# Sixteen units of one modulation matrix move from the first stage into a feed-forward

## The reference, cut to what matters

```python
def ada_params(cvec, w, b):                 # w_ada_2: 1024 x 9216, b_ada_2: 9216
    m = jax.nn.silu(cvec) @ w + b
    return m.reshape(cvec.shape[0], N_ADA, 1, D_MODEL)    # nine vectors of 1024

def half_ffn(h, shift, scale, gate, g_pre, g_post, w13, w2):
    u = modulate_2(rmsnorm_2(h, g_pre), shift, scale)
    return h + 0.5 * gate * rmsnorm_2(swiglu(u, w13, w2), g_post)
```

## Time and profile before

| | |
|---|---|
| median of the runs | 2324.3 us |
| the profiled execution's own time | 2324.03 us |
| its span | 2322.7 us |
| TensorE busy | 1988.2 us (86%) |
| VectorE busy | 1008.7 us (43%) |
| ScalarE busy | 735.0 us (32%) |
| GpSimd busy | 42.6 us (2%) |
| moved by DMA | 672.03 MB, mean 289 GB/s |
| mean granted TensorE clock | 0.93 |

### The profile page before, as it was taken

One profiled execution on the slowest core, in us unless ns is written; L12 is line 12 of the kernel. 1 busy time (PEld: TensorE's weight loads), 2 busy tenths in 40 slices (PEclk: granted clock), 3 DMA queues, 4 the chain that ended last, 5 costly groups with the idle time before them and its releaser, 6 DMA issues.

```text
span 2322.7 us, 28401 instructions
## 1 busy us (share of the span) xinstructions
PE 1988.2 (86%) x11830; PEld 1307.0 (56%) x11830; DVE 1008.7 (43%) x1713; ACT 735.0 (32%) x1196; POOL 42.6 (2%) x47
## 2 busy tenths in 40 slices
PE   6999877877877777877788789989999899999997
PEld 3646413433333333332444378868999788785786
DVE  3544222212222221222533277667664767653486
ACT  4323211101111111112210054454654554543365
POOL 0000000000000000000000000000000000000010
PEclk9999789899889998988889999999999999999999
DMA  9977999999999999999999965535345555350430
GB/s 390 414 306 266 408 377 413 414 413 414 413 414 416 415 413 415 414 411 409 414 403 410 410 207 181 186 102 169 113 141 177 164 178 186 98 199 19 145 119 19
DMA packets 210432, 672.03 MB, mean 289 GB/s; under 512 B 11504, under 2 KB 134512, under 8 KB 152192
## 3 DMA queue, kind: packets, MB, share of 16 engines
q1 hardware_dynamic: 210304, 670.21, 74.8%
HBM read 669.12 MB, written 1.05 MB: 289 GB/s over the span
## 4 chain that ended last, share of the span: by engine, by line
PE 50%; DMA 34%; DVE 11%; ACT 4%; issue 2%; SPq 0%; POOL 0%; DVEq 0%; ACTq 0%; POOLq 0%
DMA ring<-in_w 25%; PE pb L232 7%; PE pb L233 7%; PE pb L234 7%; PE pb L240 7%; DMA ring<-in_w_a 5%; PE pb L241 3%; PE pb L1852 3%; DVE WB L339 3%; DMA ring<-in_w_in 3%; PE pb L1877 2%; PE pb L782 2%; ACT WB L333 1%; DMA ring<-in_w_mod 1%; PE pb L1836 1%
## 5 line engine op out<-in xcount | busy, mean ns | idle before, releaser
L339 DVE TENSOR_TENSOR WB<-ring,WB 128x1024 fp32r<-128x1024 f32 (+3 forms) x370 | 426.1, 1193 | 463.9 <-ACT WB L333 463.6
L333 ACT ACTIVATE WB<-ring 128x1024 fp32r<-128x1024 f32 (+3 forms) x370 | 361.6, 1026 | 799.2 <-DMA ring<-in_w_a 466.0
L1852 PE MATMUL pb<-ring,big 128*32 128x512 f32 x2048 | 302.7, 684 | 139.9 <-DMA ring<-in_w 124.2
L232 PE MATMUL pb<-HHL,WB 128*128 128x256 f32 (+1 forms) x976 | 292.0, 299 | 11.7 <-DVE WB L339 4.3
L233 PE MATMUL pb<-HHL,WB 128*128 128x256 f32 (+1 forms) x976 | 283.0, 290 | 0.0
L234 PE MATMUL pb<-HHL,WB 128*128 128x256 f32 (+1 forms) x976 | 282.5, 289 | 0.0
L240 PE MATMUL pb<-HHL,WB 128*128 128x512 f32 x704 | 250.0, 400 | 1.9 <-DVE tmpT L649 1.5
L1852 PEld LDWEIGHTS pb<-ring,big 128*32 128x32 f32 x2048 | 47.3, 114 | 360.1 <-DMA ring<-in_w 268.3
L232 PEld LDWEIGHTS pb<-HHL,WB 128*128 128x128 f32 x976 | 194.0, 199 | 35.8 <-issue 21.3
L1877 PE MATMUL pb<-ring,big 128*32 128x512 f32 x1024 | 172.5, 673 | 48.4 <-DMA ring<-in_w 40.4
L241 PE MATMUL pb<-HHL,WB 128*128 128x256 f32 x704 | 197.3, 280 | 0.0
(11 more groups left out here) (467 smaller groups left out, 2265.0 us busy)
## 6 DMA issues: line engine op xcount, KB each, us to landing
ring<-in_w SPq DMA_DIRECT2D x384, 1024.0 KB, 16.4
ring<-in_w_a SPq DMA_DIRECT2D x66, 1024.0 KB, 13.2
ring<-in_w_in SPq DMA_DIRECT2D x38, 1024.0 KB, 10.2
ring<-in_w_ada SPq DMA_DIRECT2D x36, 1024.0 KB, 9.9
ring<-in_w_b SPq DMA_DIRECT2D x33, 1024.0 KB, 5.0
ring<-in_w_mod SPq DMA_DIRECT2D x24, 1024.0 KB, 12.0
ring<-in_w_out SPq DMA_DIRECT2D x8, 1024.0 KB, 6.3
ring<-in_b_w_in SPq DMA_DIRECT2D x8, 1024.0 KB, 6.4
```

Of the source, the lines that this page charges most:

```text
L232: pe.matmul(o, l[0], r[0], start=start, stop=False)
L333: act.activation(WB[:, c % 2, 0, x:y], flat[:, x:y], ACT.Copy).then_inc(*A(("high", c, z)))
L339: dve.tensor_tensor(WB[:, c % 2, 1, x:y], flat[:, x:y], WB[:, c % 2, 0, x:y].bitcast(F32), ALU.subtract).then_inc(*V(("low", c, z), *([("f ...
L1852: e = pe.matmul(PB[half][32 * j:32 * j + 32, :], xeT[:, kk, 32 * x:32 * x + 32], s[:, 512 * j:512 * j + 512], start=kk == 0, stop=kk == 7)
```

## The change

`w_ada_2`'s columns 0 to 5119 stay where they are: two vectors of 8 units and the 4 units of `TWO`, now columns 4096 to 5119. The other 4096 columns, 16 units of 128 rows, are loaded in `fa`, three behind every four chunks. ScalarE multiplies a unit in place by its rows' conditioning values (the first unit of each half straight into a total), GpSimd adds it to the total, and when all eight are in, TensorE sums the total over the partitions with a matrix of ones, ScalarE copies the bank, TensorE picks, and VectorE adds the bias and forms the scales. This is done twice, for two halves b of 2048 columns. A freed slot is now given back by GpSimd. In the attention's projection chunks the number of units behind a chunk is taken from `FILL`. The router's first bank changes from 6 to 3. The diff, cut to its core:

```diff
-    ADA = [("ada", nb) for nb in range(5)]
-    TWO = ("ada", 4)
+    ADA = [("ada", nb) for nb in range(3)]
+    TWO = ("ada", 2)
+    FILL = (1, 1, 1, 1, 2, 2, 1)
...
+    LATE_AT = {1 + 4 * k // 3: k for k in range(16)}
+
+    def sp_late(sp, t):
+        if t not in LATE_AT:
+            return
+        b, u = divmod(LATE_AT[t], 8)
...
+            load(sp, ("late", b, u), late_columns(b, u), 2048)
...
+    def late_total(b):
+        return ((big[:, 6656:8192], 0, 1536), (mraw[:, :], 1536, 2048)) if b else ((big[:, 3584:5632], 0, 2048),)
+
+    def act_late(act, t):
...
+        act.wait_ge(*landed(("late", b, u)))
+        if u:
+            act.activation(part, part, ACT.Copy, scale=cs[:, 1, u, 0:1]).then_inc(*A(("late", b, u)))
+            return
...
+    def pool_late(pool):
+        for b in range(2):
+            for u in range(1, 8):
+                pool.wait_ge(*at("late", b, u))
+                pool.wait_ge(*(at("late_total", b, u - 1) if u > 1 else at("late", b, 0)))
+                for total, x, y in late_total(b):
+                    pool.tensor_tensor(total, total, slot(("late", b, u))[:, x:y], ALU.add).then_inc(
+                        *G(*([("late_total", b, u), ("free", ("late", b, u))] if y == 2048 else [])))
+
+    def pe_late_sum(pe, b):
+        pe.wait_ge(*at("late_total", b, 7))
+        pe.wait_ge(*at("summed", "fa", 9 if b else 6, 0 if b else 1, 0 if b else 1))
+        for j in range(4):
...
+            e = pe.matmul(late_bank(b)[32 * j:32 * j + 32, :], ones[:, 0:32], total[:, 0:512] if b and j == 3 else total[:, 512 * j:512 * j + 512],
+                          start=True, stop=True)
+        e.then_inc(*P(("late_sum", b)))
+
+    def pe_late_pick(pe, b):
+        pe.wait_ge(*at("late_raw", b))
...
+    def act_late_raw(act, b):
+        act.wait_ge(*at("late_sum", b))
...
+        act.activation(fa.tmp[0], late_bank(b)[:, :], ACT.Copy).then_inc(*A(("late_raw", b)))
...
# attention, in all engines' programs
-                steps(g2, 3)
+                steps(g2, FILL[q - 1])
...
-            steps(g2, 3)
+            steps(g2, FILL[3 + q])
...
# sp_half
             load_chunk(sp, c)
+            if F is fa:
+                sp_late(sp, c - F.s0)
# pe_half
+                    if F is fa and (p, q, f) == (7, 1, 0):
+                        pe_late_sum(pe, 0)
+                    if F is fa and (q, f) == (1, 1) and p in (8, 10):
+                        pe.wait_ge(*at("late_raw" if p == 8 else "late_out", 0))
...
+            if F is fa and p == 9:
+                pe_late_pick(pe, 0)
# act_half, inside the loop over q, behind the split and the Silu
+                if F is fa:
+                    act_late(act, 2 * p + q)
...
+            elif F is fa and p == 8:
+                act_late_raw(act, 0)
...
+            if F is fa and n == 9:
+                act_late_raw(act, 1)
# dve_half
+                if F is fa and (p, q) == (10, 0):
+                    dve_late_out(dve, 0)
+                if F is fa and (p, q) == (7, 1):
+                    dve.wait_ge(*at("late_sum", 0))
# pool_program
             pool_turn2(pool, name)
+            if name == "fa":
+                pool_late(pool)
```

More of the change, by code:

```diff
@@ new lines, in late_total @@
+    def late_total(b):
+        return ((big[:, 6656:8192], 0, 1536), (mraw[:, :], 1536, 2048)) if b else ((big[:, 3584:5632], 0, 2048),)
+    def act_late(act, t):
+        if t not in LATE_AT:
+            return
+        b, u = divmod(LATE_AT[t], 8)
+        part = slot(("late", b, u))
+        act.wait_ge(*landed(("late", b, u)))
+        if u:
+            act.activation(part, part, ACT.Copy, scale=cs[:, 1, u, 0:1]).then_inc(*A(("late", b, u)))
+            return
+        for total, x, y in late_total(b):
+            act.activation(total, part[:, x:y], ACT.Copy, scale=cs[:, 1, u, 0:1]).then_inc(
+                *A(*([("late", b, u), ("free", ("late", b, u))] if y == 2048 else [])))
@@ new lines, in pe_late_sum @@
+    def pe_late_sum(pe, b):
+        pe.wait_ge(*at("late_total", b, 7))
+        pe.wait_ge(*at("summed", "fa", 9 if b else 6, 0 if b else 1, 0 if b else 1))
+        for j in range(4):
+            total = late_total(b)[j // 3 if b else 0][0]
+            e = pe.matmul(late_bank(b)[32 * j:32 * j + 32, :], ones[:, 0:32], total[:, 0:512] if b and j == 3 else total[:, 512 * j:512 * j + 512],
[3 more added lines that the diff above has]
+        pe.wait_ge(*at("late_raw", b))
+        if b == 0:
+            pe.wait_ge(*at("summed", "fa", 8, 1, 1))
+        for i in range(4):
+            e = pe.matmul(late_bank(b)[:, 8 * i:8 * i + 8].rearrange("p (j c) -> p j c", c=2), fa.tmp[0][:, 128 * i:128 * i + 128],
+                          ident.rearrange("p (j c) -> p j c", j=4)[:, :, 0:2], start=True, stop=True)
+        e.then_inc(*P(("late_pick", b)))
@@ new lines, in pe_late_last, with dve_late_out @@
+    def pe_late_last(pe):
+        yield
+        yield
+        pe_late_sum(pe, 1)
+        yield
+        yield
+        yield
+        pe_late_pick(pe, 1)
+        yield
+    def act_late_raw(act, b):
+        act.wait_ge(*at("late_sum", b))
+        if b:
+            act.wait_ge(*at("late_pick", 0))
+        act.activation(fa.tmp[0], late_bank(b)[:, :], ACT.Copy).then_inc(*A(("late_raw", b)))
+    def dve_late_out(dve, b):
+        dve.wait_ge(*at("late_pick", b))
+        for c, j0, nj in ((48, 0, 4),) if b else ((40, 0, 2), (64, 2, 2)):
+            dve.tensor_tensor(mcol2[:, c:c + 4 * nj, :].rearrange("p (j i) c -> p i j c", i=4),
+                              late_bank(b)[:, 0:32].rearrange("p (i j c) -> p i j c", i=4, c=2)[:, :, j0:j0 + nj, :],
+                              col("b_ada_2", c, 4 * nj).rearrange("p (j i) -> p i j", i=4)[:, :, :, None].to_broadcast([128, 4, nj, 2]),
+                              ALU.add).then_inc(*V(*([("late_out", b)] if c != 40 else [])))
+        dve.wait_ge(*at("late_out", b))
+        if b:
+            dve.scalar_tensor_tensor(AB2[:, 32:40], mcol2[:, 56:64, 0], 1.0, ng(4), ALU.add, ALU.mult).then_inc(*V())
+        else:
+            dve.tensor_tensor(AB2[:, 56:64], mcol2[:, 40:48, 0], ng(3), ALU.mult).then_inc(*V())
+            dve.scalar_tensor_tensor(AB2[:, 64:72], mcol2[:, 64:72, 0], 0.5, ng(5), ALU.mult, ALU.mult).then_inc(*V())
@@ L2289, in dve_half @@
                 sp_.upto(F.s0 + 23 + n // 2)
+            if F is fa and n == 16:
+                dve_late_out(dve, 1)
             if F is fb and n == 5:
```

31 lines of the change are left out of this document (19 added, 12 removed).

## The result

The kernel became slower: 2367.83 us median (2366.93 to 2373.32, four runs) against 2324.05 us, a ratio of 1.0189 with a 95% interval of 1.0175 to 1.0203. The profiled execution took 2366.93 us with a span of 2365.5 us.

A forecast was written before the change was run, and what follows sets the result against it. TensorE was taken to bound the first stage and `fa`'s first half, the DMA engines the experts' stage. 2324.0 - 11.3 + 3.8 + 2.9 + 36.2 = 2355.6, forecast 2355 us, own range 2338 to 2367.

The forecast's parts named there:

- rival D: In `fa`: the forecast's waits, plus TensorE's clock falling behind them, another 12 to 15 us; 2369 us, chance 0.13.
- The first stage: Before the experts: fewer units and vector ends on TensorE's path, less some new waits; -11.3 us.
- rivals B and C: First stage returns the transfers' whole 40.6 us: B with contention, 2326 us, 0.07; C with contention hidden, 2290 us, 0.07.
- Sums and picks: In `fa`: two sums by ones and two picks add matmuls to TensorE, +3.8 us with gaps.
- the copy's wait: In `fa`, round 8: TensorE waits for ScalarE's copy of the first sum's bank, +2.9 us.
- GpSimd's additions: In `fa`: additions shut out VectorE's operations with two SBUF inputs, so TensorE waits; 36.2 us, bounds 0 to 64.
- the walk: Step-by-step timing of a pair of `fa` chunks, used to place and size the waits behind GpSimd's additions, 36.2 us.
- the first low halves of the five even chunks: In `fa`, t = 2, 6, 10, 14, 18: VectorE's first low half stands behind an addition; 14.3 us together.
- The second low half: In `fa`'s even chunks: another addition goes between the two halves, 4.3 us at three of five; 12.9 us.
- The odd chunks: In `fa`: product pair and low half wait for the addition together, 1 us for each of nine; 9 us.
- Rival A: In `fa`: additions slip into VectorE's gaps, 29% of 123 us, so contention is hidden; 2319 us, chance 0.13.
- The signs: Trace signs: experts start near 235 us, `fa`'s first half 165 instead of 123, L339's mean above 2, GpSimd over 64 more.

The follow-up runs named there:

- no_late: The kernel after without the late units (transfers, products, additions, sums, picks), leaving only the first stage's part: 2310.7 us, ratio 0.9933.
- light_units: The kernel before with ten projection-loop units still transferred but multiplied in one 8-column matmul instead of four of 512: 2322.6 us, ratio 0.9987.
- tiny_add: The kernel after with each GpSimd addition cut to 8 columns, all else kept: 2321.6 us, ratio 0.9991.
- write_only: The kernel after with each GpSimd addition replaced by three memsets of the same columns, which read nothing: 2320.3 us, ratio 0.9984.
- order: The kernel after with ScalarE's late unit put ahead of the Silu on even chunks instead of behind it: 2348.8 us, ratio 1.0102.
- split_add: The kernel after with each GpSimd addition made in four pieces of 512 columns: 2350.9 us, ratio 1.0112.
- combined: The kernel after with additions in four pieces, late unit ahead of the Silu, first sum's copy one round earlier: 2332.2 us, ratio 1.0042.
- vec_add: The kernel after with one VectorE operation per late unit instead of a ScalarE pass and a GpSimd addition: 2324.8 us, ratio 1.0002.
- vec_spread: As vec_add, with the second half's units spread over later chunks and the first copy behind round 7: 2321.7 us, ratio 0.9992.

## Why the prediction was right, and where its sizes were off

**What was right, and how closely.** The change costs time, and the cost is TensorE waiting for low halves that stand behind GpSimd's additions: that is the prediction's mechanism, and the runs show it. The size was less good. The measured 2367.8 us lies 13 us above the 2355, and 0.8 us above the forecast's own range of 2338 to 2367; only rival D's share of the range holds it. That D's 2369 us came within 2 us is in part luck: D has 36.2 us of waits and 12 to 15 of clock behind a gain of 11.3, the trace has 30, 20 and 17.7.

**The first stage: -11.3 booked.** no_late has -12.1 in medians. In the profiled pair the experts started 13.2 us earlier, and the experts' stage was another 4.5 us shorter, which I had put at nothing. The transfers' whole 40.6 us (rivals B and C) did not come: the DMA share from 101 to 205 us fell to 0.76. But my reason was too simple. I read the ring's 110.5 us of waits as "TensorE sets the pace"; light_units took 9 us off TensorE alone and the experts moved by 4.0. The change could gain more since it took both the units and their transfers; that is argued, no run takes the transfers alone. A wait of the queue on slots says that the ring is full at that moment and not that the transfers would be hidden everywhere. A slip without weight: the TensorE row from 230.23 is six units of four matmuls and not "twelve instructions' worth".

**Sums and picks +3.8, the copy's wait +2.9.** The new matmuls took 5.0 us (3.1 for the sums, 1.9 for the picks), and the wait 4.0 us in the kernel after, 2.8 in tiny_add. tiny_add and write_only, which hold all of this and the transfers, have `fa` 8.8 and 7.0 us above before, 6.7 booked.

**GpSimd's additions: 36.2 booked.** This is the term that carries the result, and its mechanism is shown by five runs: take the additions' length away (46 us back), keep GpSimd busy without reads (48 us back), cut them (17 us), reorder them (19 us), do them on VectorE (43 us). The waits sum to less than booked: 23.7 us on L339, 3.4 us more at L529 than before, 2.0 in front of L232, 29.1 us in all. Most of them stood where the walk had put them. The two of t = 2 are shown above; these are the two of t = 6, those of t = 10, 14 and 18, and one on an odd chunk:

```profile
1397.79 0.47 PE L240 MATMUL pb<-HHL,WB 128*128 128x512 f32 x1 [3.49 <-DVE WB L339]
1403.16 0.79 PE L240 MATMUL pb<-HHL,WB 128*128 128x512 f32 x1 [3.08 <-DVE WB L339]
1432.17 0.47 PE L240 MATMUL pb<-HHL,WB 128*128 128x512 f32 x1 [4.60 <-DVE WB L339]
1460.77 0.77 PE L240 MATMUL pb<-HHL,WB 128*128 128x512 f32 x1 [3.31 <-DVE WB L339]
1494.38 0.77 PE L240 MATMUL pb<-HHL,WB 128*128 128x512 f32 x1 [1.50 <-DVE WB L339]
1503.48 0.47 PE L240 MATMUL pb<-HHL,WB 128*128 128x512 f32 x1 [1.88 <-DVE WB L339]
```

With the 2.65 and 2.88 us of t = 2 above, the first low halves of the five even chunks cost 15.6 us (14.3 booked). The second low half held TensorE only twice, at t = 2 and 6, for 2.9 and 3.1 us: 6.0 where three of 4.3, 12.9 us, were booked. That is the part of the walk that was mis-sized. The odd chunks cost 7.6 of the 9 booked, but mostly not at L339: the product pair waited, and with it L529, whose diagonals stand in VectorE's line behind a product (which no step had), and L232, which takes the product itself.

**The clock: booked as a rival at 0.13, and it came true beside the forecast.** `fa` minus its idle time is 215.8 us in the kernel after and 196.0 in tiny_add with the same matmuls, 19.8 us at clock 0.89 against 0.97. Rival D had 12 to 15. Two 20 us windows of `fa` in the kernel after, one with the waits of t = 2 and one without a wait:

```profile
1348.12:1368.12 20.00, 14.48 (x60) 11.50 (x59) 16.28 (x11) 8.82 (x9) 9.92 (x2) 0.74 0.64 222
1548.12:1568.12 20.00, 20.00 (x90) 16.51 (x90) 11.66 (x17) 9.82 (x16) 0.00 (x0) 1.00 0.00 0
```

So the additions' price is 30 us of waiting (the 29.1 and 1.2 more on the copy) and about 20 us of slower matmuls, 50 where I had 36; by the medians of after and tiny_add it is 46. That the clock falls because of the waits is read from their coming together, no run parts the two. It held in every run with full additions on GpSimd: against tiny_add's 9.7 us idle and 196.0 busy, `order` has 18.8 us more idle and 14.4 more busy, `split_add` 18.9 and 10.9, `combined` 9.2 and 7.1, so each microsecond of waiting came with 0.6 to 0.8 of slower matmuls.

**Sum.** -17.7 + 58.8 + 1.8 for -11.3 + 42.9. The sign and the mechanism were right; the waits were sized a quarter too high (36.2 for 29.1), and the slower clock that came with them, which belongs to the forecast and not to a rival, was left out of it. The two errors have opposite signs.

**Rival A (hidden in VectorE's gaps)** did not come about: VectorE had 29% idle, and TensorE still waited nine times behind L339, 23.7 us in all. vec_add is its counterpart, with 37 us more on VectorE in one order and 0.5 us of waiting behind L339.

**The signs.** The experts started at 233.01 ("near 235"), and GpSimd was busy 70.8 us more ("over 64"). The first half of `fa` grew from 127.6 to 181.6 us, where I had 123 growing to 165. L339's mean, said to rise above 2 us, was 1.63 over the whole of `fa`, whose second matrix's chunks meet almost no addition.

What stays open: why the experts' stage was 4.5 us shorter. From the first expert to `fa`'s transposes it lasted 1094.7 to 1097.9 us in the eleven other traces, 1099.6 in the kernel before's only one, and light_units, which changes nothing there, has 1097.8; so a part of it is scatter. Open too is what lowers the clock in the heads. And vec_spread's 3 us need more runs than were made.

## What to carry to other kernels

Before work is given to an idle GpSimd, look at VectorE's two-input SBUF operations in the same stretch: a 4.5 us addition stood in front of the next one for its whole length here, and VectorE's program order carried the wait to TensorE. Fused VectorE operations, 2.3 us for a unit of 128x2048, made the kernel 43 us faster than a ScalarE pass and a GpSimd addition for each unit, on engines with room to spare. Where TensorE bounds, add to a forecast wait the slower clock that comes with it, here 0.6 to 0.8 of the wait.

## What the runs showed of the hardware that was not expected

- GpSimd memsets of 128x2048 f32 took 1.81 us and held up neither L339 (1221 ns, as with GpSimd idle) nor the product pair, while additions of the same tile took 4.5 us and more, and one L339 under them 5.55 us.
- With 56 pieces of 1.3 us in place of additions of 4.5 us, the longest L339 fell from 5.55 to 2.31 us but its mean only from 1630 to 1506 ns, and the longest piece took 2.29 us: both engines wait for each other, one operation at a time.
- Identical instructions ran in the first stage at a granted clock of 0.93 in one execution and 0.57 to 0.73 in another between 140 and 180 us, and the latter fell some 11 us behind.
